# Spreading a scaled one-hot on GpSimd while a coefficient matrix is filled, with codes read from PSUM, four PSUM banks and a token-major store

## The reference, cut to what matters

```python
u = peer_u[eidx]                                   # 128 chosen rows of 1024 per token
a = gelu(einsum('nhkd,nd->nhk', u, xb))            # one dot product per choice
coef = g * a                                       # g: softmax of the chosen scores
return einsum('nhk,nhkd->nd', coef, peer_v[eidx])  # weighted sum of the chosen rows of peer_v
```

## Time and profile before

| | before |
|---|---|
| runs | 4554.2, 4540.98, 4552.7 us; median 4552.7 us |
| profiled execution | 4541.82 us, span 4540.2 us |
| granted TensorE clock, mean | 0.932 |
| busy: PE / PEld | 3830.6 us (84%) / 2304.7 us (51%) |
| busy: DVE / ACT / POOL | 2595.6 us (57%) / 724.2 us (16%) / 1499.0 us (33%) |
| HBM traffic over the span | 235 GB/s |

### The profile page before, as it was taken

One profiled execution on the slowest core, in us unless ns is written; L12 is line 12 of the kernel. 1 busy time (PEld: TensorE's weight loads), 2 busy tenths in 40 slices (PEclk: granted clock), 3 DMA queues, 4 the chain that ended last, 5 costly groups with the idle time before them and its releaser, 6 DMA issues.

```text
span 4540.2 us, 40362 instructions
## 1 busy us (share of the span) xinstructions
PE 3830.6 (84%) x14392; PEld 2304.7 (51%) x14392; DVE 2595.6 (57%) x5470; ACT 724.2 (16%) x897; POOL 1499.0 (33%) x1247
## 2 busy tenths in 40 slices
PE   7999997999987990027999869999679998699998
PEld 6878874555557990025444354444454343544443
DVE  3111104434323888989978699797898786920000
ACT  3111112333421110024000050000330001500000
POOL 0000000000000477753656524656336564331100
PEclk9999997999998995568999989999899999899999
DMA  4222116233314799875999948999669998486654
GB/s 167 84 82 102 65 54 209 101 111 118 126 60 135 241 320 320 268 254 187 391 405 397 382 145 337 404 403 403 229 240 393 402 399 328 137 301 204 204 162 139
DMA packets 321866, 1068.09 MB, mean 235 GB/s; under 512 B 51665, under 2 KB 54801, under 8 KB 319601
## 3 DMA queue, kind: packets, MB, share of 16 engines
q0 software_dynamic: 179520, 654.00, 40.0%
q1 hardware_dynamic: 137712, 391.66, 23.9%
q10 hardware_dynamic: 4480, 20.45, 1.2%
HBM read 1003.20 MB, written 62.78 MB: 235 GB/s over the span
## 4 chain that ended last, share of the span: by engine, by line
PE 38%; DVE 13%; DMA 12%; POOL 3%; issue 2%; ACT 1%; SPq 0%; ACTq 0%; DVEq 0%
PE pair L1731 31%; DMA e_vr<-in_peer_v 10%; DVE e_ur L1527 5%; POOL e_ur L1275 3%; DVE e_sc L1607 3%; PE pair L1713 3%; PE pair L1685 2%; PE pair L1664 2%; DVE e_sc L1612 2%; DMA e_ur<-in_peer_u,e_eidx 2%; DVE e_oh L1596 0%; DVE e_sc L1434 0%; DVE e_oh L1601 0%; DVE e_oh L1598 0%; DMA e_sc<-sc_d 0%
## 5 line engine op out<-in xcount | busy, mean ns | idle before, releaser
L1731 PE MATMUL pair<-e_vr,e_region 128*128 128x512 f32 x4096 | 1807.5, 597 | 45.2 <-DMA e_vr<-in_peer_v 43.7
L1275 POOL DMA_INDIRECT e_ur<-in_peer_u,e_eidx x1088 | 1383.2, 1271 | 1252.9 <-DVE e_dots L1527 930.5
L1527 DVE CUSTOM_DVE_ANT_0 e_ur<-e_ur,e_h 128x1024 f32<-128x1024 f32 x1088 | 1304.3, 1222 | 297.2 <-DMA e_ur<-in_peer_u,e_eidx 288.3
L1731 PEld LDWEIGHTS pair<-e_vr,e_region 128*128 128x128 f32 x4096 | 762.1, 190 | 1079.7 <-issue 839.5
L1713 PE MATMUL pair<-e_sc 128*128 128x128 f32 x2048 | 339.7, 325 | 178.8 <-DVE e_sc L1607 149.4
L1713 PEld LDWEIGHTS pair<-e_sc 128*128 128x128 f32 x2048 | 304.9, 231 | 214.5 <-DVE e_sc L1607 181.5
L400 PE MATMUL pair<-w_hi,h_hi 128*128 128x512 f32 (+1 forms) x936 | 365.8, 391 | 0.7 <-issue 0.6
L400 PE MATMUL pair<-w_lo,h_hi 128*128 128x512 f32 (+1 forms) x936 | 365.1, 390 | 0.0
L400 PE MATMUL pair<-w_hi,h_lo 128*128 128x512 f32 (+1 forms) x936 | 364.6, 390 | 0.0
L1383 ACT ACTIVATE e_region<-pair 128x512 f32<-128x512 f32 x256 | 272.4, 1070 | 247.9 <-PE pair L1713 239.2
L148 DVE TENSOR_SCALAR e_n<-e_n 128x1 f32<-128x1 f32 (+1 forms) x9 | 1.4, 153 | 533.4 <-ACT e_n L143 533.4
(11 more groups left out here) (215 smaller groups left out, 2979.7 us busy)
## 6 DMA issues: line engine op xcount, KB each, us to landing
e_vr<-in_peer_v SPq DMA_DIRECT2D x512, 512.0 KB, 6.7
w<-in_w_in POOLq DMA_DIRECT2D x13, 2048.0 KB, 9.4
proj<-out_sb SPq DMA_DIRECT2D x104, 256.0 KB, 2.0
e_ur<-in_peer_u,e_eidx POOLq DMA_INDIRECT x1088, 8.3
V<-proj POOLq DMA_DIRECT2D x36, 256.0 KB, 3.0
gates<-proj SPq DMA_DIRECT2D x8, 1024.0 KB, 4.9
e_region<-in_w_pq SPq DMA_DIRECT2D x4, 2048.0 KB, 15.1
sc_d<-e_region ACTq DMA_DIRECT2D x16, 512.0 KB, 5.9
```

The lines of the kernel that those rows point to most:

```text
L1275: pool.indirect_dma_start(ur[:, m % U_RING, :], None, peer_u[0], bass.IndirectOffsetOnAxis(ap=eidx[:, n % 3, k:k + 1], axis=0))\
L1527: dve.tensor_tensor_reduce(ur[:, m % U_RING, :], ur[:, m % U_RING, :], h2[:, n % 2, :], 1.0, 0.0, ALU.mult, ALU.add, dots[:, n % 2, k:k + ...
L1731: last = pe.matmul(acc[t][:, c], dense[:, t, i, :], vr[:, no % V_RING, c], start=False, stop=True, skip_group_check=True)
```

## The change

The multiply that makes `hot1` moves from DVE to GpSimd, into the queue that issues the gathers: from gather 7 of the tile on, two batches follow each gather. `oh16` and `oh8` get two buffers and a counter `hot_rdy`. `kT` is no longer a tile in SBUF: the transposes' result stays in PSUM (`pair[0]`), DVE reads it there, and ACT's copies and `kT_rdy` go. The freed bank becomes a fourth `cb_ps`. `dense` is laid out (tile, token, first half): ACT writes it without a step, and PE's weight loads in the stream read it with a step of 128 elements (512 bytes).

```diff
@@ -1118,15 +1118,15 @@
     GELU_CUBE, GELU_ROOT = 0.044715, float(np.sqrt(2.0 / np.pi))
     acc = [pair[0], pair[1], pair[2]]
     q_ps, s_ps = [pair[1], pair[3]], pair[2]
-    cb_ps = [pair[2][:, 0:BANK], pair[2][:, BANK:], pair[3][:, 0:BANK]]
-    kt_ps = pair[3][:, BANK:]
+    cb_ps = [pair[2][:, 0:BANK], pair[2][:, BANK:], pair[3][:, 0:BANK], pair[3][:, BANK:]]
+    kT = pair[0][:, :].rearrange("p (t i n) -> p t i n", t=2, n=P)
     with ExitStack() as ctx:
         sb = lambda n, s, d=F32: ctx.enter_context(nc.sbuf_tensor("e_" + n, s, d))
         region = sb("region", [P, 2 * KEYS * P])
-        dense = region[:, :].rearrange("p (t i n) -> p t i n", t=2, n=P)
+        dense = region[:, :].rearrange("p (t n i) -> p t n i", t=2, n=P)
         wpq = region[:, 0:16384].rearrange("p (k n) -> p k n", k=KD)
         pkT = region[:, 16384:18432].rearrange("p (s k) -> p s k", k=P)
         hT = region[:, 18432:20480].rearrange("p (b k c) -> p b k c", b=2, c=P)
@@ -1159,14 +1159,13 @@
         dots = sb("dots", [P, 2, SLOTS])
         ge = sb("ge", [P, SLOTS])
         coef = sb("coef", [P, 2, SLOTS])
-        kT = sb("kT", [P, 2, 4, P])
-        oh16 = sb("oh16", [P, SMALL, 16])
-        oh8 = sb("oh8", [P, SMALL, 8])
+        oh16 = sb("oh16", [P, 2, SMALL, 16])
+        oh8 = sb("oh8", [P, 2, SMALL, 8])
         n3 = sb("n3", [P, 3, 4])
         names = ("keys_in keys_turned keysT_rdy q_rdy qT_rdy s_rdy sc_rdy sc_in y_out u_used s_used "
                  "gf_in v_used gf_used route gates_rdy best_rdy exp_rdy gelu arg_rdy gelu_exp coef_rdy diag_rdy norm "
-                 "x3_rdy sq3_rdy y_rdy prep prep_rdy keys_rdy kT_rdy small o2_rdy o1_rdy cb_mm filled").split()
+                 "x3_rdy sq3_rdy y_rdy prep prep_rdy keys_rdy small hot_rdy o2_rdy o1_rdy cb_mm filled").split()
         s = {n: sem("c_" + n) for n in names}
         quarters = [slice(i * PQ_W // 4, (i + 1) * PQ_W // 4) for i in range(4)]
         w_in = [sem(f"c_w_in{i}") for i in range(4)]
@@ -1287,10 +1286,28 @@
                                             bass.IndirectOffsetOnAxis(ap=eidx[:, LAST % 3, k:k + 1], axis=0))\
                         .then_inc(u_in[m % U_RING], 16)
+                def hots1(g, m):
+
+                    at = m * BATCH
+                    q = g * (2 * P // SMALL) + at // SMALL
+                    if at % SMALL == 0:
+                        pool.wait_ge(s["hot_rdy"], 2 * q + 2)
+                    if m >= 2:
+                        pool.wait_ge(s["cb_mm"], g * BATCHES + m - 1)
+                    own = slice(at % SMALL, at % SMALL + BATCH)
+                    big = oh8[:, q % 2, own, :].rearrange("p n (h a) -> p n h a", a=1)
+                    low = oh16[:, q % 2, own, :].rearrange("p n (a l) -> p n a l", a=1)
+                    pool.tensor_tensor(hot1[:, m % 2].rearrange("p n (h l) -> p n h l", l=16),
+                                       big.to_broadcast([P, BATCH, 8, 16]), low.to_broadcast([P, BATCH, 8, 16]),
+                                       ALU.mult).then_inc(s["o1_rdy"], 1)
+
                 for n in range(NT):
                     pool.wait_ge(s["gates_rdy"], n + 1)
                     for k in range(dots_of(n)):
                         gather_u(n, k)
+                        if n >= 2 and n % 2 == 0 and 0 <= k - 1 - U_RING < BATCHES // 2:
+                            hots1(n // 2 - 1, 2 * (k - 1 - U_RING))
+                            hots1(n // 2 - 1, 2 * (k - 1 - U_RING) + 1)
                 for k in range(S_DOTS):
                     gather_v(k)
@@ -1374,14 +1391,11 @@
                     if g == 0:
                         for half in sc_out:
                             act.wait_ge(half, 16 * (NT - 1))
-                    for t in range(2):
-                        act.wait_ge(s["keys_rdy"], 2 * g + t + 1)
-                        act.activation(kT[:, t], in_blocks(kt_ps), ACT.Copy).then_inc(s["kT_rdy"], 1)
                     for m in range(BATCHES):
                         t, at = divmod(m * BATCH, P)
                         act.wait_ge(s["cb_mm"], g * BATCHES + m + 1)
-                        act.activation(dense[:, t, :, at:at + BATCH].rearrange("p i n -> p n i"),
-                                       cb_ps[m % 3].rearrange("p (n i) -> p n i", n=BATCH), ACT.Copy)\
+                        act.activation(dense[:, t, at:at + BATCH, :],
+                                       cb_ps[m % 4].rearrange("p (n i) -> p n i", n=BATCH), ACT.Copy)\
                             .then_inc(s["filled"], 1)
                 for m in range(HALVES):
@@ -1585,32 +1599,28 @@
                 def hots(g, m):
                     t, at = divmod(m * BATCH, P)
+                    q = g * (2 * P // SMALL) + m * BATCH // SMALL
+                    iota = C["iota"].rearrange("p (a k) -> p a k", a=1)
                     if at == 0:
-                        dve.wait_ge(s["kT_rdy"], 2 * g + t + 1)
+                        dve.wait_ge(s["keys_rdy"], 2 * g + t + 1)
                     if at % SMALL == 0:
-                        if g or m:
-                            dve.wait_ge(s["o1_rdy"], g * BATCHES + m)
+                        if q >= 2:
+                            dve.wait_ge(s["o1_rdy"], (q - 1) * (SMALL // BATCH))
                         tok = slice(at, at + SMALL)
                         hi, lo, cf = [kT[:, t, i, tok].rearrange("p (n a) -> p n a", a=1) for i in (0, 1, 3)]
-                        iota = C["iota"].rearrange("p (a k) -> p a k", a=1)
-                        small.then(dve.tensor_tensor(oh16[:], lo.to_broadcast([P, SMALL, 16]),
-                                                     iota[:, :, 0:16].to_broadcast([P, SMALL, 16]), ALU.is_equal))
-                        small.then(dve.tensor_tensor(oh8[:], hi.to_broadcast([P, SMALL, 8]),
+                        dve.tensor_tensor(oh16[:, q % 2], lo.to_broadcast([P, SMALL, 16]),
+                                          iota[:, :, 0:16].to_broadcast([P, SMALL, 16]), ALU.is_equal)\
+                            .then_inc(s["hot_rdy"], 1)
+                        small.then(dve.tensor_tensor(oh8[:, q % 2], hi.to_broadcast([P, SMALL, 8]),
                                                      iota[:, :, 0:8].to_broadcast([P, SMALL, 8]), ALU.is_equal))
                         small.wait()
-                        small.then(dve.tensor_tensor(oh8[:], oh8[:], cf.to_broadcast([P, SMALL, 8]), ALU.mult))
-                        small.wait()
+                        dve.tensor_tensor(oh8[:, q % 2], oh8[:, q % 2], cf.to_broadcast([P, SMALL, 8]), ALU.mult)\
+                            .then_inc(s["hot_rdy"], 1)
                     if m >= 2:
                         dve.wait_ge(s["cb_mm"], g * BATCHES + m - 1)
                     i2 = kT[:, t, 2, at:at + BATCH].rearrange("p (n a) -> p n a", a=1)
-                    iota = C["iota"].rearrange("p (a k) -> p a k", a=1)
                     dve.tensor_tensor(hot2[:, m % 2], i2.to_broadcast([P, BATCH, KEYS]),
                                       iota.to_broadcast([P, BATCH, KEYS]), ALU.is_equal).then_inc(s["o2_rdy"], 1)
-                    own = slice(at % SMALL, at % SMALL + BATCH)
-                    big = oh8[:, own, :].rearrange("p n (h a) -> p n h a", a=1).to_broadcast([P, BATCH, 8, 16])
-                    low = oh16[:, own, :].rearrange("p n (a l) -> p n a l", a=1).to_broadcast([P, BATCH, 8, 16])
-                    dve.tensor_tensor(hot1[:, m % 2].rearrange("p n (h l) -> p n h l", l=16), big, low, ALU.mult)\
-                        .then_inc(s["o1_rdy"], 1)
                 for p in range(PARTS):
                     routing(0, p)
@@ -1697,20 +1707,18 @@
                         n = 2 * g + t
                         pe.wait_ge(s["prep_rdy"], n + 1)
                         pe.wait_ge(s["coef_rdy"], n + 1)
-                        if n > 0:
-                            pe.wait_ge(s["kT_rdy"], n)
                         for i in range(3):
-                            pe.transpose(kt_ps[:, i * P:(i + 1) * P], part[:, i, :], C["ident"])
-                        pe.transpose(kt_ps[:, 3 * P:4 * P], coef[:, t, :], C["ident"]).then_inc(s["keys_rdy"], 1)
+                            pe.transpose(kT[:, t, i, :], part[:, i, :], C["ident"])
+                        pe.transpose(kT[:, t, 3, :], coef[:, t, :], C["ident"]).then_inc(s["keys_rdy"], 1)
                     if g == 0:
                         pe.wait_ge(s["sc_rdy"], HALVES)
                     for m in range(BATCHES):
                         pe.wait_ge(s["o2_rdy"], g * BATCHES + m + 1)
                         pe.wait_ge(s["o1_rdy"], g * BATCHES + m + 1)
-                        if m >= 3:
-                            pe.wait_ge(s["filled"], g * BATCHES + m - 2)
+                        if m >= 4:
+                            pe.wait_ge(s["filled"], g * BATCHES + m - 3)
                         for i in range(BATCH):
-                            last = pe.matmul(cb_ps[m % 3][:, i * P:(i + 1) * P], hot2[:, m % 2, i, :],
```

(3 more changed lines are left out.)

## The result

The changed kernel takes 4576.06 us (median of 5 runs, 4569.82 to 4584.72), the kernel before, run beside it, 4541.68 us (5 runs, 4538.71 to 4554.2). The ratio is 1.0069, with a 95% interval from 1.0051 to 1.0088: slower by about 31 us. The profiled execution lasts 4576.06 us with a span of 4574.5. The direction is the one forecast; the size is about a third of the +88 us of the sum.

A forecast was written before the change was run, and what follows sets the result against it. DVE was taken to set the fill's step, transfers or PE to bind the streams; GpSimd's queue with the dot would add 88 us, ACT save 2: 4541.8 + 88 - 2 = 4628, forecast 4630 us, range 4480 to 4715.

The forecast's parts named there:

- the sum: Whole kernel: 4541.8 us, plus 88 for longer fill steps, minus 2 for ACT's last copies, gives 4628 us.
- behind dots at up to 2 us: Sign in a fill after the change: GpSimd's gathers, held by DVE's dots, take up to 2 us.
- near 0.60: Fill: ACT's copy, written without a step, goes from 1.07 to about 0.60 us; 2 us gained over four fills.
- dots longer than 1.22 us: Sign in a fill: dots longer than 1.22 us, or starting late, where a GpSimd multiply runs.
- Rival 1: Fill: multiply reads beside the dot, GpSimd's queue needs 3.48 us a step, 4482 us in all; chance 0.12.
- a step of 4.62 us: Fill: gather 0.94, issue 0.30, two multiplies of 1.12 and dot 1.14 in a row; 0.69 us above 3.93.
- the overlap of gather and dot: Fill step: gather 0.94, its issue 0.30 and the dot 1.14 us were added in full, one after another.
- X: Fill: duration of one multiply on GpSimd, taken as two operand passes, 1.12 us.
- the small one-hots: Fill: made in DVE's slack of 4.62 - 2.72 us; if that cover went, 0.4 us more a step.
- the 3.93 us of the prediction: Fill before the change: DVE's mean step, 3.55 us plus a quarter of 1.51 for the small one-hots.
- rival 2: Fill: quick multiply of 0.61 us; 4498 us with exclusion, 4385 without; chance 0.07.
- The weight loads: Streams: PE's loads with a 512-byte step go from 190 ns to near 0.34 us, stay covered, cost taken as 0.

The follow-up runs named there:

- h2_psum: Changed kernel, but ACT copies `h2` into PSUM once per fill and the fill's dots read it there: 4459.59 us, ratio 0.9808.
- codes_sbuf: Changed kernel, but ACT copies the wide compare's codes into SBUF, so the compare reads two SBUF operands: 4623.82 us, ratio 1.0166.
- split_pair: Changed kernel with the gather placed between a step's two multiplies in GpSimd's queue: 4610.03 us, ratio 1.0134.
- early_small: Changed kernel with the small one-hots of the next 32 tokens made two steps before they are needed: 4569.43 us, ratio 1.0042.

## Why the prediction was right in direction and three times too large

**What held.** The mechanism is the one forecast: dot and multiply exclude one another, the dot adds to GpSimd's queue, and so the fill becomes longer although DVE has less to do. `h2_psum` shows it from one side (the dot let go, 28 us off a fill) and `codes_sbuf` from the other (the compare held too, 11 us on). Gathers "behind dots at up to 2 us" (1.78), ACT's copy "near 0.60" (597 ns), and "dots longer than 1.22 us" came as written. Rival 1 (a multiply that reads beside the dot) falls with the dot at 2.89 us; what it would have given is what `h2_psum` made possible. That the time came within 54 us of the forecast is in part luck: of the measured +34 us the fills, the only place where the sum had a loss, bring 23.5 where it had 88, and 16.6 come from the streams and the way to them, which it had put at nothing.

The Trainium skill, page "SBUF — State Buffer", section "Who interferes with whom", says that the one that has the shared read holds it for its whole instruction, and that a DVE instruction with at most one SBUF input, outside the 2-port performance modes, does not contend. By the first rule, the trace agrees for a single instruction: a multiply of 1.34 us behind a dot, a dot of 1.57 us behind one multiply in `split_pair`. The rule as the prediction used it, whichever starts first goes first, does not carry over to the multiply behind: the dot at 2649.70 waits for the second multiply too, which starts after it. There the measurement decides. By the second rule, the trace agrees: compares of 683 ns and, in `h2_psum`, dots of 1.21 us beside the multiplies.

**What was off: the terms of the step.** The sum had a step of 4.62 us; the step without small one-hots measured 4.03.

- The step of the prediction that failed is the overlap of gather and dot. It put the gather's 0.94 us, its issue of 0.30 and the dot's 1.14 one after another, 2.38 us. It had itself read that a gather beside a dot ends 0.89 us after it. Measured is 1.03 (dot) + 0.89 (what is left of the gather) + 0.04 (gaps) = 1.96 us: the gather's issue and its beginning pass while the dot runs. That is 0.42 us per step, 54 us in all.
- X, a multiply: taken 1.12 us, measured 1.03 to 1.06 (two in 2.07). 0.17 us per step, 22 us in all.

These are 0.59 us x 128 = 76 us too much. The other way went the small one-hots: the prediction had them covered by DVE's slack, but that slack went into held dots. GpSimd waits 0.64 us for them once in four steps, 0.16 us a step where the prediction had named 0.4 for a lost cover, and the mean over four steps is 4.17 us.

The step before was not quite the 3.93 us of the prediction either: by the starts of the compares, 6 of the second fill's steps take 3.83 to 4.03 us instead of 3.55, and at 2619.46 DVE's compare has waited 0.38 us for PE. From the first compare of the second fill to that of its last step, 31 steps, it is 123.2 us before and 128.2 after: 5.0 of the 5.8 us of the window. The rest lies at the fill's edges and was not followed up.

The page "GPSIMD Engine Reference" of the Trainium skill, section 3.1, has a ratio of 1.96 to DVE for 2048 elements. The measured 1.06 us for 512 is about 1.55 times DVE's 0.68; here the measurement decides, and the prediction's 1.12 was nearer than the 1.34 of that ratio.

**The order.** "So the dot waits for that multiply's end, and then the second multiply waits for the dot" was wrong: the dot waits for both. The length of the step is the same either way, so the sum did not suffer; but for this reason PE's idle time went on being ended by DVE, where the prediction had GpSimd. The sign that was to tell of rival 2 ("DVE still the one that ends PE's idle time") would have misled a reader: the compare is late because of the dot, and the dot because of GpSimd. So would the sign of rival 1: the multiplies have the same length with and without a dot beside them (1.05 to 1.08 us in the second fill, none near 2.2), but because it is always the dot that waits. And DVE did not become idle: it is busy for 126.7 of the 135.4 us, waiting inside its dots.

**The weight loads.** Forecast near 0.34 us and covered; measured 296 ns. The streams were to stay within 2 us, and the cost was put at 0; this was somewhat wrong (473.2 and 561.5 us in the windows, against 469 and 557). The twelve transfer-bound streams of the four profiled kernels with the old order last 462.2 to 470.8 us, with a mean of 466.5; the 21 of the seven with the new order 464.4 to 475.2, with a mean of 469.4. So about 3 us a stream, though the means of single kernels overlap (465.1 to 468.7 and 467.5 to 470.9), and little or nothing in the last one, which PE binds (551.7 to 553.4 us with the old order, 551.8 to 554.1 with the new). A longer load ahead of the first matmul of a block that came late would do it (0.106 us each); that was only argued, and no run separates it.

**Nothing forecast: the way from a fill to its stream.** Eight identity matmuls open a stream. The timeline after the fourth fill has them as:

```profile
3999.42 6.20 PE L1731 MATMUL pair<-e_vr,cst 128*128 128x512 f32 x8 [0.69 <-ACT e_region L1397]
```

Before, the same eight took 3.70 us from 3969.54 on. The granted clock in 3999.5 to 4003.5 is 0.50, the 1.2 GHz level, and 1.00 (2.4 GHz) in 3969.6 to 3973.2 before. In the stretch just ahead, 3992.0 to 3999.4, it is 0.88 with PE busy for 4.7 of 7.4 us; before, in 3962.0 to 3969.5, 1.00 with 4.5 of 7.5 us. So PE had done about the same there, and these rows do not tell what lowered the clock. Two of four stream starts were longer in this way, by 2.0 (granted clock 0.63 from 2754.4 to 2760.1) and 3.1 us. From the fill's last copy to the stream's first product the fourth start takes 6.6 to 8.6 us in the eight kernels with the multiply on GpSimd, and 4.9 to 6.0 in the three without; in these profiles it goes with the multiply and not with the order of the matrix, and the cause stays open.

## What to carry to other kernels

Before moving work from DVE to GpSimd, go through what DVE still does at the same time: an instruction with two SBUF operands, as the dot and `codes_sbuf`'s compare, can add to GpSimd's queue (the dot 0.83 us a step here, 4.03 against 3.20), and a copy of one operand in PSUM can decide whether the move pays (a ratio of 1.0069 without it, 0.9808 with it). When two engines exclude one another, write the step as one line of work and add only what is left of each piece after the piece ahead of it; what a held gather does ahead of its wait is paid already. And the releaser that ends an idle time may itself be late: look at how long its own predecessor took against the same instruction undisturbed.

## What the runs showed of the hardware that was not expected

- A dot that waits for SBUF does not get in between two GpSimd multiplies that stand back to back: 2.89 us instead of 1.22.
- A dot that starts 0.39 us or more into a gather waits for the multiplies that directly follow the gather, though it starts ahead of them: 3.38 us in `split_pair`, up to 3.76 in `early_small`. One that starts 0.06 to 0.22 us into it does not wait (1.21 to 1.22 us).
- A GpSimd multiply of two broadcast operands in SBUF, 128 x 512 f32, takes 1.03 to 1.06 us, about 1.55 times DVE's 0.68.
- A weight load whose columns lie 512 bytes apart takes 296 ns instead of 190, and ACT's copy with the same step 1070 instead of 597 ns: 1.56 and 1.79 times.
- The first matmuls of a stream ran at a granted clock of 0.50 in one place where those of the kernel before, after about the same busy time of PE (4.7 of 7.4 us and 4.5 of 7.5), ran at 1.00: 6.20 us for eight instead of 3.70.
